# Laying out and loading the conditioning weights of a decoder step in another way

## The reference

```python
def adaln(c, w_ada, b_ada):
    m = jax.nn.silu(c) @ w_ada + b_ada          # (9, 1024) @ (1024, 6144)
    return jnp.split(m[:, None, :], 6, axis=-1)

def modulate(x, g, shift, scale):
    return rms_norm(x, g) * (1 + scale) + shift

def decoder_layer(x, c, pos, attend, lambda_init, p):
    sh1, sc1, g1, sh2, sc2, g2 = adaln(c, p['w_ada'], p['b_ada'])
    h = modulate(x, p['norm1_g'], sh1, sc1)
    z = h @ p['w_in']
    ...
    x = x + g1 * mix
    h2 = modulate(x, p['norm2_g'], sh2, sc2)
    x = x + g2 * peer(h2, ...)
```

## Time before, and the profile

| | us |
|---|---|
| median of 3 runs (lowest, highest) | 5044.74 (5025.33, 5049.15) |
| the profiled execution, its own time | 5042.86 |
| its span in the trace | 5041.2 |
| first instruction of the second phase (L214) starts | 126.93 |
| PE busy in the block products (L130) | 90.6 |

### The profile page before, as it was taken

How to read it: one execution, slowest core, us unless ns; L and a number is a source line. 1 busy time by engine, 2 the same in 40 slices (tenths; PEclk the granted TensorE clock), 3 DMA queues, 4 the chain that set the end, 5 groups by cost and what they waited for, 6 DMA issues and landing times.

```text
span 5041.2 us, 47478 instructions
## 1 busy us (share of the span) xinstructions
PE 3057.7 (61%) x16593; PEld 1823.3 (36%) x16593; DVE 2533.0 (50%) x5702; ACT 605.4 (12%) x1241; POOL 2654.6 (53%) x2173
## 2 busy tenths in 40 slices
PE   7689999888266754666864655244344354533344
PEld 1566777567255322433432433022232111310000
DVE  0785060341887776466777455322334455557411
ACT  0211151221001320001421000000000000000000
POOL 0322222000467777677777777433434677777675
PEclk9799999899678777877876877666666667666665
DMA  6322221234999999999999999999999999999998
GB/s 206 114 83 84 74 95 60 68 130 163 323 365 376 393 389 401 389 401 384 396 363 393 399 401 382 366 336 360 358 342 360 400 400 385 378 400 408 360 364 301
DMA packets 690974, 1556.41 MB, mean 309 GB/s; under 512 B 49982, under 2 KB 357631, under 8 KB 689658
## 3 DMA queue, kind: packets, MB, share of 16 engines
q0 software_dynamic: 317856, 1161.96, 59.9%
q1 hardware_dynamic: 372908, 391.81, 23.4%
HBM read 1497.13 MB, written 65.23 MB: 310 GB/s over the span
## 4 chain that ended last, share of the span: by engine, by line
DMA 23%; POOL 21%; PE 15%; SPq 10%; issue 8%; DVE 4%; ACT 0%; POOLq 0%; DVEq 0%; ACTq 0%
DMA v_rows<-in_peer_v,expertsT 13%; POOL v_rows L972 11%; POOL u_rows L963 10%; PE ps_y L1240 5%; SPq L837 5%; DMA k_pages<-in_cache_kT 4%; PE ps_bank L1100 3%; PE ps_bank L1094 2%; DMA subkeys<-in_peer_subkeysT 2%; SPq L844 2%; DMA scores<-scratch_scores 2%; DMA u_rows<-in_peer_u,experts 1%; PE ps_bank L1018 1%; DVE u_rows L1807 1%; SPq L769 1%
## 5 line engine op out<-in xcount | busy, mean ns | idle before, releaser
L1807 DVE CUSTOM_DVE_ANT_0 u_rows<-u_rows,h_rows 128x1024 f32<-128x1024 f32 x1056 | 1288.4, 1223 | 1130.4 <-DMA u_rows<-in_peer_u,experts 938.5
L963 POOL DMA_INDIRECT u_rows<-in_peer_u,experts x1024 | 1235.2, 1206 | 755.5 <-DVE experts L1760 389.4
L972 POOL DMA_INDIRECT v_rows<-in_peer_v,expertsT x1056 | 1171.9, 1110 | 869.8 <-PE ps_y L1240 587.5
L1240 PE MATMUL ps_y<-v_rows,w_columns 128*32 128x512 f32 x4224 | 841.5, 939 | 1175.6 <-DMA v_rows<-in_peer_v,expertsT 1139.0
L1240 PEld LDWEIGHTS ps_y<-v_rows,w_columns 128*32 128x32 f32 x4224 | 169.2, 148 | 1661.5 <-issue 1659.2
L355 PE MATMUL ps_z<-w_in_high,hT_high 128*128 128x512 f32 (+1 forms) x1008 | 401.8, 399 | 29.4 <-ACTq L379 27.2
L355 PE MATMUL ps_z<-w_in_high,hT_low 128*128 128x512 f32 (+1 forms) x1008 | 398.8, 396 | 0.0
L355 PE MATMUL ps_z<-w_in_low,hT_high 128*128 128x512 f32 (+1 forms) x1008 | 397.3, 394 | 0.0
L330 POOL CAST w_in_high<-w_in_buf 128x4096 fp32r<-128x4096 f32 x13 | 47.5, 3657 | 491.6 <-PE ps_z L355 463.1
L1100 PE MATMUL ps_bank<-turned_a,weights 128*128 128x256 f32 (+1 forms) x1280 | 281.4, 382 | 34.5 <-DMA subkeys<-in_peer_subkeysT 32.7
L1094 PE MATMUL ps_bank<-weights,turned_a 128*128 128x256 f32 (+1 forms) x1152 | 273.4, 399 | 12.8 <-DMA weights<-in_w_out 8.3
(11 more groups left out here) (200 smaller groups left out, 3613.7 us busy)
## 6 DMA issues: line engine op xcount, KB each, us to landing
k_pages<-in_cache_kT SPq DMA_DIRECT2D x128, 512.0 KB, 12.9
v_pages<-in_cache_v SPq DMA_DIRECT2D x128, 512.0 KB, 8.5
weights<-in_peer_w_q SPq DMA_DIRECT2D x40, 1024.0 KB, 16.6
w_in_buf<-in_w_in POOLq DMA_DIRECT2D x14, 2048.0 KB, 9.1
scratch_z<-z_out SPq DMA_DIRECT2D x112, 256.0 KB, 2.0
w_ada_buf<-in_w_ada POOLq DMA_DIRECT2D x12, 2048.0 KB, 8.5
weights<-in_w_att_out SPq DMA_DIRECT2D x20, 1024.0 KB, 19.8
weights<-in_w_gm_out SPq DMA_DIRECT2D x20, 1024.0 KB, 18.7
```

The costliest lines, as they stand in the source:

```text
L963: pool.indirect_dma_start(ur[:, n % RU, :], None, g.peer_u, bass.IndirectOffsetOnAxis(ap=col, axis=0)).then_inc(s_ur[n % RU], 16)
L972: pool.indirect_dma_start(vr[:, n % RV, :], None, g.peer_v, bass.IndirectOffsetOnAxis(ap=idxT[:, t % 3, k:k + 1], axis=0)).then_inc(s_vr[n ...
L1240: last = nc.tensor.matmul(ps_y[32 * j:32 * (j + 1), b:b + CB], wcol[:, base:base + 32], vr[:, (V0[t] + i + j) % RV, b:b + CB], start=r == ...
L1807: nc.vector.tensor_tensor_reduce(ur[:, n % RU, :], ur[:, n % RU, :], hrow[:, t % 2, :], 1.0, 0.0, ALU.mult, ALU.add, a[:, s:s + 1]).then_i ...
```

## The change

The host lays `w_ada` out as [block][partition][k][column], so that a block is one piece of HBM and each partition's part of it is one run of 16 KB. There are eight buffers. SP issues the loads of the even blocks and ACT those of the odd ones; POOL issues the small loads of bias, gain and lambda vectors, after it has set three tiles to zero. A group is now GB = 4 blocks, and there are NQ = 3 groups. In a group PE puts block j on columns 32j to 32j+31 of its array, with `cT` padded from 9 to 32 columns, and goes round the four blocks inside each k. The result of a group is one PSUM bank with block j on partitions 32j and up, so that DVE adds the bias of four blocks with one instruction of 128 x 512, and each scale part is one instruction of 64 x 512. The stores are 12 DMAs of 9 x 512, four behind each group.

```diff
--- before.py
+++ after.py
@@ -60,16 +60,18 @@
 def adaln_phase(nc, g):
 
     NC = 1 + NSEQ
-    WB = 2
+    WB = 8
+    GB = 4
     NB = MODS * D // CB
+    NQ = NB // GB
     with ExitStack() as ctx:
         sb = lambda name, shape, dt=F32: ctx.enter_context(nc.sbuf_tensor(name, shape, dt))
         c_rows = sb("c_rows", [NC, D])
         c_silu = sb("c_silu", [NC, D])
-        cT = sb("cT", [P, KD, NC])
-        bias = sb("ada_bias", [NC, MODS * D])
-        gain = sb("ada_gain", [NC, 2, D])
-        mod = sb("mod_rows", [NC, MODS * D])
+        cT = sb("cT", [P, KD, 32])
+        bias = sb("ada_bias", [P, NQ, CB])
+        gain = sb("ada_gain", [P, 2, CB])
+        mod = sb("mod_rows", [P, NQ, CB])
         ident = sb("ident_a", [P, P])
         w = sb("w_ada_buf", [P, WB, KD, CB])
...
-        ps_m = ctx.enter_context(nc.psum_tensor("ps_mod", [P, 2, CB], F32))
-        s_in, s_silu, s_ct, s_ctc, s_mm, s_mod, s_out = [
-            g.sem(n) for n in ("a_inputs", "a_silu", "a_cT_psum", "a_cT", "a_product", "a_mod", "a_stored")]
+        ps_m = ctx.enter_context(nc.psum_tensor("ps_mod", [P, NQ, CB], F32))
+        s_in, s_silu, s_ct, s_ctc, s_mm, s_mod, s_out, s_zero, s_gain = [
+            g.sem(n) for n in ("a_inputs", "a_silu", "a_cT_psum", "a_cT", "a_product", "a_mod", "a_stored", "a_zeroed", "a_gained")]
         s_c = g.sem("a_conditioning")
         s_w = [g.sem(f"a_weights{b}") for b in range(WB)]
-        w_view = g.w_ada.rearrange("(k p) n -> p k n", p=P)
+        SCALES = {0: slice(64, 128), 2: slice(0, 64)}
         with nc.Block() as block:
             @block.sync
             def _(sp):
                 sp.dma_start(c_rows[0:1, :], g.c_prompt).then_inc(s_c, 16)
                 sp.dma_start(c_rows[1:NC, :], g.c_sample).then_inc(s_c, 16)
                 sp.dma_start(ident[:], g.ident).then_inc(s_c, 16)
-                sp.dma_start(bias[:], g.b_ada.broadcast_to([NC, MODS * D])).then_inc(s_in, 16)
-                sp.dma_start(gain[:, 0, :], g.norm1_g.broadcast_to([NC, D])).then_inc(s_in, 16)
-                sp.dma_start(gain[:, 1, :], g.norm2_g.broadcast_to([NC, D])).then_inc(s_in, 16)
-                for n, v in enumerate((g.lambda_q1, g.lambda_k1, g.lambda_q2, g.lambda_k2)):
-                    sp.dma_start(lvec[:, n, :], v.broadcast_to([P, DH])).then_inc(s_in, 16)
-                sp.wait_ge(s_mod, NB + 2)
-                sp.dma_start(g.mod, mod[:]).then_inc(s_out, 16)
-                sp.wait_ge(s_out, 16)
+                for b in range(0, NB, 2):
+                    if b >= WB:
+                        sp.wait_ge(s_mm, (b - WB) // GB + 1)
+                    sp.dma_start(w[:, b % WB], g.w_ada[b]).then_inc(s_w[b % WB], 16)
+                for q in range(NQ):
+                    sp.wait_ge(s_gain if q in SCALES else s_mod, (1 if q == 0 else 2) if q in SCALES else q + 1)
+                    for j in range(GB):
+                        n = GB * q + j
+                        sp.dma_start(g.mod[:, n * CB:(n + 1) * CB], mod[32 * j:32 * j + NC, q, :]).then_inc(s_out, 16)
+                sp.wait_ge(s_out, 16 * NB)
+
+            @block.scalar
+            def _(act):
+                for b in range(1, NB, 2):
+                    if b < WB:
+                        act.dma_start(w[:, b % WB], g.w_ada[b]).then_inc(s_w[b % WB], 16)
+                act.wait_ge(s_c, 48)
+                nc.scalar.activation(c_silu[:], c_rows[:], ACT.Silu).then_inc(s_silu, 1)
+                for b in range(WB + 1, NB, 2):
+                    act.wait_ge(s_mm, (b - WB) // GB + 1)
+                    act.dma_start(w[:, b % WB], g.w_ada[b]).then_inc(s_w[b % WB], 16)
+                act.wait_ge(s_ld, 2)
+                nc.scalar.activation(ldot[:], ldot[:], ACT.Exp).then_inc(s_le, 1)
 
             @block.gpsimd
             def _(pool):
-                for b in range(WB):
-                    pool.dma_start(w[:, b], w_view[:, :, b * CB:(b + 1) * CB]).then_inc(s_w[b], 16)
-                with pool.Fori(1, NB // WB) as i:
-                    for b in range(WB):
-
-                        pool.wait_ge(s_mm, i * WB + (b + 1 - WB))
-                        pool.dma_start(w[:, b], w_view[:, :, bass.ds(i * (WB * CB) + b * CB, CB)]).then_inc(s_w[b], 16)
-
-            @block.scalar
-            def _(act):
-                act.wait_ge(s_c, 48)
-                nc.scalar.activation(c_silu[:], c_rows[:], ACT.Silu).then_inc(s_silu, 1)
-                act.wait_ge(s_ld, 2)
-                nc.scalar.activation(ldot[:], ldot[:], ACT.Exp).then_inc(s_le, 1)
+                nc.gpsimd.memset(cT[:], 0.0).then_inc(s_zero, 1)
+                nc.gpsimd.memset(bias[:], 0.0).then_inc(s_zero, 1)
+                nc.gpsimd.memset(gain[:], 0.0).then_inc(s_zero, 1)
+                pool.wait_ge(s_zero, 3)
+                for q in range(NQ):
+                    for j in range(GB):
+                        n = GB * q + j
+                        pool.dma_start(bias[32 * j:32 * j + NC, q, :], g.b_ada[:, n * CB:(n + 1) * CB].broadcast_to([NC, CB])).then_inc(s_in, 16)
+                for n, (src, js) in enumerate(((g.norm1_g, (2, 3)), (g.norm2_g, (0, 1)))):
+                    for c, j in enumerate(js):
+                        pool.dma_start(gain[32 * j:32 * j + NC, n, :], src[:, c * CB:(c + 1) * CB].broadcast_to([NC, CB])).then_inc(s_in, 16)
+                for n, v in enumerate((g.lambda_q1, g.lambda_k1, g.lambda_q2, g.lambda_k2)):
+                    pool.dma_start(lvec[:, n, :], v.broadcast_to([P, DH])).then_inc(s_in, 16)
 
             @block.tensor
             def _(pe):
@@ -124,44 +140,36 @@
                     last = nc.tensor.transpose(ps_t[:, k * NC:(k + 1) * NC], c_silu[:, k * P:(k + 1) * P], ident[0:NC, 0:NC])
                 last.then_inc(s_ct, 1)
                 pe.wait_ge(s_ctc, 1)
-
-                def block_product(b):
+                for q in range(NQ):
+                    for j in range(GB):
+                        n = GB * q + j
+                        pe.wait_ge(s_w[n % WB], 16 * (n // WB + 1))
                     for k in range(KD):
-                        last = nc.tensor.matmul(ps_m[0:NC, b, :], cT[:, k, :], w[:, b, k, :], start=k == 0, stop=k == KD - 1)
+                        for j in range(GB):
+                            last = nc.tensor.matmul(ps_m[32 * j:32 * (j + 1), q, :], cT[:, k, :], w[:, (GB * q + j) % WB, k, :], start=k == 0, stop=k == KD - 1)
                     last.then_inc(s_mm, 1)
-                for b in range(WB):
-                    pe.wait_ge(s_w[b], 16)
-                    block_product(b)
-                with pe.Fori(1, NB // WB) as i:
-                    for b in range(WB):
-                        pe.wait_ge(s_w[b], i * 16 + 16)
-
-                        pe.wait_ge(s_mod, i * WB + (b + 1 - WB))
-                        block_product(b)
 
             @block.vector
             def _(dve):
+                dve.wait_ge(s_zero, 1)
                 dve.wait_ge(s_ct, 1)
-                nc.vector.tensor_copy(cT[:].rearrange("p k c -> p (k c)"), ps_t[:, 0:KD * NC]).then_inc(s_ctc, 1)
-                dve.wait_ge(s_in, 112)
-                with dve.Fori(0, NB // WB) as i:
-                    for b in range(WB):
-                        dve.wait_ge(s_mm, i * WB + (b + 1))
-                        cols = bass.ds(i * (WB * CB) + b * CB, CB)
-                        nc.vector.tensor_tensor(mod[:, cols], ps_m[0:NC, b, :], bias[:, cols], ALU.add).then_inc(s_mod, 1)
-
+                nc.vector.tensor_copy(cT[:, :, 0:NC], ps_t[:, 0:KD * NC].rearrange("p (k c) -> p k c", c=NC)).then_inc(s_ctc, 1)
+                dve.wait_ge(s_in, 16 * (NB + 4 + 4))
                 for n in range(2):
                     nc.vector.tensor_tensor_reduce(lprod[:, n, :], lvec[:, 2 * n, :], lvec[:, 2 * n + 1, :], 1.0, 0.0,
                                                    ALU.mult, ALU.add, ldot[:, n:n + 1]).then_inc(s_ld, 1)
+                for q in range(NQ):
+                    dve.wait_ge(s_mm, q + 1)
+                    nc.vector.tensor_tensor(mod[:, q, :], ps_m[:, q, :], bias[:, q, :], ALU.add).then_inc(s_mod, 1)
+                    if q in SCALES:
+                        rows, n = SCALES[q], q // 2
+                        dve.wait_ge(s_mod, q + 1)
+                        nc.vector.scalar_tensor_tensor(out=mod[rows, q, :], in0=mod[rows, q, :], scalar=1.0, in1=gain[rows, n, :],
+                                                       op0=ALU.add, op1=ALU.mult).then_inc(s_gain, 1)
                 dve.wait_ge(s_le, 1)
                 nc.vector.tensor_tensor(ldif[:], ldot[:, 0:1], ldot[:, 1:2], ALU.subtract).then_inc(s_lam, 1)
                 dve.wait_ge(s_lam, 1)
                 nc.vector.tensor_scalar(g.lam[:], ldif[:], LAMBDA_INIT, None, ALU.add).then_inc(s_lam, 1)
-                dve.wait_ge(s_mod, NB)
-                for n in range(2):
-                    part = mod[:, (3 * n + 1) * D:(3 * n + 2) * D]
```

(5 more changed lines are left out.)

## The result

The changed kernel takes 4992.25 us in the median of 5 runs (4982.10 to 4999.22), the kernel before 5032.77 us in the median of 5 (5008.54 to 5049.15). The ratio is 0.9913, with a 95% interval of 0.9894 to 0.9933: faster by 0.9%. The profiled execution is the one of 4992.25 us.

The account below looks back on a forecast made before the run. PE bounds the first phase before the change, the loads after it. The terms 69.1 + 1.5 + 10.0 + 1.5 + 1.1 + 5.9 give 89.1 us in place of 126.93, so 5005.0 us, range 4987 to 5021.

Parts of the forecast that it names:

- The bound moves from PE to the loads: First phase: PE sets the time before, the block loads after; only the third group's products stay on the path.
- The stream, 400 GB/s and an end at 69.1: Block loads of the first phase: 25.17 MB at 400 GB/s take 62.9 us, ending at 69.1 us.
- the rate does not rise: Rival on the block loads: they stay at 373 GB/s and take 67.5 us, total 5009.6 us; chance 0.22.
- The first group at 28.7 and refills with 9 us of slack: First four blocks there at 28.7 us, products end at 38.7, other loads keep the DMA engines busy until 48.1.
- a gap in the DMA row: Sign of being wrong, in the first phase's loads: the four refills come only after a gap; no size given.
- Products, 10.0 us for the third group: PE's last 64 passes in the first phase: 22 at the slow pace, 42 at the fast, 10.0 us.
- DVE, 1.5 us: Behind the first phase's last product: start 0.15, addition 0.68, half of 1.2 for a scaling; 1.5 us in all.
- The stores, 1.1 + 5.9 us: End of the first phase: three more store issues, 1.1 us, then 5.9 us from last issue to next phase.
- Small loads costing nothing on the path: POOL's zeroing and 20 small loads end at about 22 us; late only beyond 58 us more.
- The column groups not running together: Rival on PE: 64 passes take 27.3 us, kernel 5037.5 us, no change; chance 0.07.
- Slow runs of 16 KB: Rival on the block loads: at 200 GB/s or below the kernel is 0.5% slower; chance 0.04.
- The gain lost elsewhere: Rival on later phases: the gather phase ends 15 to 20 us later, total about 5023 us; chance 0.09.

Follow-up runs that it names:

- e1: Changed kernel with a group's four blocks multiplied one after the other; second phase starts at 110.18 us instead of 83.96.
- e4: Changed kernel with four block buffers instead of eight; second phase starts at 103.77 us instead of 83.96.
- e2: Changed kernel with the host's old weight layout, runs of 2 KB instead of 16 KB; second phase starts at 87.79 us instead of 83.96.
- e3: Changed kernel with all twelve block loads issued by SP, none by ACT; second phase starts at 82.23 us instead of 83.96.
- e5: Changed kernel plus 44 unread products (88 passes) between second and third group; second phase starts at 80.94 us instead of 83.96.
- e6: Kernel before the change with its last store of 9 x 6144 cut into three of 9 x 2048; second phase starts at 124.84 us instead of 126.93.
- e7: Changed kernel with all twelve stores held until the last scaling; second phase starts at 86.13 us instead of 83.96.

## Why the prediction was right, point by point

- **The mechanism and the total.** Forecast 5005.0 us and faster by over 0.5%, with 4987 to 5021; measured 4992.25. By the medians the gain is 40.5 us where 37.8 was forecast. The second phase was to start at 89.1 us and starts at 83.96. Of the 12.75 us between forecast and median, 5.1 lie there; the profiled run's third phase is 8.1 us shorter than that of the profile before. That part is chance: it lies inside the third phase's scatter, and no step of the prediction foresaw it.
- **The bound moves from PE to the loads.** Right: PE waits 33.7 us before its three groups, and POOL no longer waits for PE at all. e1 and e4 show that the whole gain needs both the overlap on PE and the room to load ahead.
- **The stream, 400 GB/s and an end at 69.1.** Near: 400 GB/s over 5 to 45 us, 428 at the end, and the third group starts at 69.06 where 70.6 was worked out. The rival that the rate does not rise is refuted as a description of the change: with 2 KB runs it stays at 380 to 395 (e2), with 16 KB runs it does not. The limit of 358 GB/s of the Trainium skill, DMA: Bandwidth & Descriptors, section Specifications, does not hold in this trace (400 GB/s for 40 us).
- **The first group at 28.7 and refills with 9 us of slack.** This step failed. It took for granted that two queues bring blocks in order. The first group started at 36.05, since ACT's queue ran ahead into blocks of the second group, and the refills were asked for when the queues were nearly empty. The prediction had named a gap in the DMA row there as a sign that it is wrong; what came is a dip to 306 GB/s at 45 to 50 us, by itself (400 - 306) x 5 / 400 = 1.2 us, an estimate. One queue has neither the late first group nor the dip (e3), but its third group starts only 0.23 us sooner, so the failed step cost next to nothing on the path. The rule of the Trainium skill, on the same page in the section Rules for kernel authors, that spreading DMAs over queues does not help bandwidth, agrees with e3: 396 GB/s with one queue over 5 to 45 us, 400 with two.
- **Products, 10.0 us for the third group.** Measured 9.91, with the first rounds slow as worked out from the earlier trace rows; e5 shows that the idle stretch is the cause.
- **DVE, 1.5 us.** 1.5 from the end of the products (78.97) to the first store (80.47).
- **The stores, 1.1 + 5.9 us.** Mis-sized: 3.5 us from the first of the last four issues to the next phase instead of 7.0. The sum kept the 5.9 us of one store of 216 KB for four that write 72 KB in narrower rows, and counted nothing for either difference. This is the largest error of the sum, 3.5 of 5.1 us; e6 and e7 leave open which difference it was.
- **Small loads costing nothing on the path.** Right in its effect, wrong in its times: POOL had issued them all by 14.3 us, but DVE could only start on them at 46.6, 1.2 us after the first group had ended. The cover held, with 32 us to spare until the third group's end instead of 58.
- **The column groups not running together.** Refuted by the pace of the groups and by e1. **Slow runs of 16 KB:** refuted by 400 to 428 GB/s. **The gain lost elsewhere:** the second phase keeps its 801 us, and the third scatters without a sign.

## What to carry to other kernels

When a load and an engine share a phase with too little room, find what each takes alone: here 192 passes of 90.6 us could become 29 because the stationary operand was 9 columns wide, and then the bytes set the time; what is left to win is what stands behind the last byte. A second queue did not add rate to full DMA engines here (400 GB/s with two, 396 with one), and it brought the blocks in an order that nobody asked for; put what is needed first on one queue, and mind small loads that stand in a queue ahead of large ones. Where a later phase scatters by as much as the gain, measure the change by a mark inside the trace.

## What the runs showed of the hardware that was not expected

- Two hardware queues with work did not share the bytes from the start: 3.29 MB for ACT's against 0.19 MB for SP's from 2 to 12 us, then half each. From 7 us on they shared by packets, 123 to 128 in 5 us, though ACT's were of 14 KB in the mean and SP's of 1.2 KB.
- Loads of 0.43 MB through POOL's queue, issued by 14.3 us, were all there only at 46.6 us beside the two full queues (69 packets and 0.04 MB from 17 to 22 us, while SP's 69 packets moved 1.03 MB), and `c_rows` and `ident`, the first on SP's queue, let ACT start at 14.05 instead of 3.38 us.
- The wait behind the last store's issue was 1.2 us with rows of 2 KB, 3.8 with 8 KB and 4.7 with 24 KB; from the first issue on, 216 KB took 5.9 to 6.4 us however they were cut.
- With runs of 2 KB a load's issue held SP for up to 14.8 us; with runs of 16 KB, on the same two queues, for 0.6 at most.
- Passes on a new column group ran beside the last ones of the old even when the program did not go round: 22.6 us for 64 passes in place of 27.3.
